# The first chunk's weights and x in two pieces instead of three, x on ScalarE's queue

## What is computed

```python
h = rmsnorm(x, norm1_g)
proj = h @ w_in + b_in                      # 1024 -> 4352 columns
qa, ka, va, qb, kb, vb, ga, gb = split(proj)
oa = neighborhood_attention(qa, ka, va, na_rpb)
ob = sliding_window_gqa(rope(qb), rope(kb), vb, swa_sinks)
merged = sigmoid(ga) * (oa @ w_up_a) + sigmoid(gb) * (ob @ w_up_b)
x = x + merged @ w_out
x = x + moe_clamped_swiglu(rmsnorm(x, norm2_g), ...)   # 32 experts, top 4
return rmsnorm(x, final_g)
```

## Time and profile before

| what | value |
|---|---|
| three timed runs | 1122.39, 1122.46, 1125.32 us |
| median | 1122.46 us |
| the profiled execution's own time | 1121.81 us |
| its span, from the first to the last instruction | 1119.6 us |
| busy in the span | TensorE 1066.8 us (95%), its weight loads 476.0, VectorE 303.2, ScalarE 114.0, GpSimd 43.1 |
| read from HBM | 434.66 MB, 389 GB/s over the span |
| chain that ended last, by engine | TensorE 74%, DMA 17%, SyncE's queue 5% |

### The profile page before, as it was taken

The page is one execution under the profiler, slowest core; times in us unless marked ns, Lnnn a source line. Parts: engine busy times, 40 slices in busy tenths (PEclk is TensorE's granted clock), DMA queues, the critical chain, the costliest instruction groups (busy, mean ns, idle before and its releaser), DMA issues.

```text
span 1119.6 us, 13354 instructions
## 1 busy us (share of the span) xinstructions
PE 1066.8 (95%) x5293; PEld 476.0 (43%) x5293; DVE 303.2 (27%) x656; ACT 114.0 (10%) x243; POOL 43.1 (4%) x44
## 2 busy tenths in 40 slices
PE   8999999999999999999999999999999999999997
PEld 7888888633333333333333333333333333333332
DVE  4356634322222222222222222222121112222213
ACT  1042520200000000000000000000000000000001
POOL 1105500000000000000000000000000000000000
PEclk9999999999999999999999999999999999999999
DMA  9953369599999999999999999999999999999996
GB/s 359 420 209 131 113 241 396 203 384 430 428 428 429 426 429 430 428 426 430 429 428 427 430 429 429 426 430 430 428 427 428 430 428 427 428 430 428 427 425 272
DMA packets 35783, 436.05 MB, mean 389 GB/s; under 512 B 4432, under 2 KB 4944, under 8 KB 6992
## 3 DMA queue, kind: packets, MB, share of 16 engines
q1 hardware_dynamic: 34752, 434.77, 92.8%
q10 hardware_dynamic: 1008, 0.95, 0.3%
HBM read 434.66 MB, written 1.05 MB: 389 GB/s over the span
## 4 chain that ended last, share of the span: by engine, by line
PE 74%; DMA 17%; SPq 5%; DVE 3%; ACT 1%; issue 1%; another core or an unknown queue 0%; POOL 0%; POOLq 0%; DVEq 0%
PE bank L862 29%; DMA ring<-in_w 17%; PE bank L924 16%; PE bank L595 5%; SPq L364 5%; PE bank L836 4%; PE bank L786 4%; PE bank L792 3%; PE bank L696 2%; PE bank L678 2%; PE bank L539 2%; DVE work L1333 2%; PE bank L591 1%; PE bank L764 1%; PE bank L517 1%; PE bank L643 1%
## 5 line engine op out<-in xcount | busy, mean ns | idle before, releaser
L862 PE MATMUL bank<-ring,work 128*64 128x512 f32 x2048 | 450.8, 593 | 18.8 <-DMA ring<-in_w 18.2
L862 PEld LDWEIGHTS bank<-ring,work 128*64 128x64 f32 x2048 | 147.7, 137 | 301.1 <-issue 273.2
L924 PE MATMUL bank<-ring,work 128*64 128x512 f32 x1024 | 234.1, 599 | 18.0 <-DVE work L1333 17.5
L924 PEld LDWEIGHTS bank<-ring,work 128*64 128x64 f32 x1024 | 67.8, 136 | 141.4 <-issue 114.9
L1323 DVE TENSOR_SCALAR work<-bank 128x512 f32<-128x512 f32 x32 | 22.1, 692 | 387.5 <-PE bank L862 387.5
L1505 ACT ACTIVATE work<-work 128x512 f32<-128x512 f32 x32 | 20.1, 630 | 722.4 <-DVE work L1323 722.4
L836 PE MATMUL bank<-work 64*128 64x512 f32 x256 | 63.6, 615 | 0.9 <-DVE work L1303 0.9
L786 PE MATMUL bank<-x2n,work 128*64 128x512 f32 x256 | 61.9, 604 | 0.8 <-DVE work L1238 0.8
L1249 DVE TENSOR_TENSOR work<-bank,vec 128x256 f32<-128x256 f32 x64 | 24.2, 419 | 134.5 <-PE bank L792 134.5
L792 PEld LDWEIGHTS bank<-cst,work 128*128 128x128 f32 x320 | 33.8, 140 | 54.2 <-issue 49.5
L595 PE MATMUL bank<-ring 128*128 128x256 f32 x240 | 54.2, 382 | 0.0
(11 more groups left out here) (194 smaller groups left out, 572.3 us busy)
## 6 DMA issues: line engine op xcount, KB each, us to landing
ring<-in_w SPq DMA_DIRECT2D x184, 2048.0 KB, 40.1
ring<-in_w_in SPq DMA_DIRECT2D x16, 1024.0 KB, 24.0
ring<-in_w SPq DMA_DIRECT2D x15, 1024.0 KB, 13.5
ring<-in_w_out SPq DMA_DIRECT2D x4, 1024.0 KB, 4.8
ring<-in_w_up_a SPq DMA_DIRECT2D x2, 1024.0 KB, 9.4
ring<-in_w_up_b SPq DMA_DIRECT2D x2, 1024.0 KB, 6.1
ring<-in_na_rpb SPq DMA_DIRECT2D x1, 1536.0 KB, 17.9
ring<-in_w SPq DMA_DIRECT2D x2, 512.0 KB, 29.4
```

Of the source, the lines that this page charges most:

```text
L862: last = pe.matmul(bank[CAP * a:CAP * (a + 1), bk, :], kT, pairs[:, pair_of(par, k // 2), at + q * 512:at + (q + 1) * 512], start=False, s ...
L924: last = pe.matmul(bank[CAP * a:CAP * (a + 1), to, :], fT, pairs[:, pair_of(par, c), at + a * 512:at + (a + 1) * 512], start=f == 0, stop= ...
```

## The change

`FIRST` has two slices, row blocks 0 to 3 and 4 to 7, 512 KB of x and 512 KB of weights each. SyncE issues the two pieces of weights only; ScalarE issues the two pieces of x, behind `vec` and ahead of the identity. The semaphores and the waits follow: two pieces for TensorE, VectorE and ScalarE instead of three.

```diff
-        xT_landed = [sem(f"xT_landed{n}") for n in range(3)]
-        first_landed = [sem(f"first_chunk_landed{n}") for n in range(2)]
+        xT_landed = [sem(f"xT_landed{n}") for n in range(2)]
+        first_landed = sem("first_chunk_landed")
...
-        FIRST = [slice(0, 2), slice(2, 4), slice(4, KD)]
+        FIRST = [slice(0, 4), slice(4, KD)]
...
             for n, ks in enumerate(FIRST):
                 cols = slice(ks.start * CW, ks.stop * CW)
-                sp.dma_start(xT[:, ks, :], xT_in[:, ks, :]).then_inc(xT_landed[n], 16)
-                sp.dma_start(ring[:, SLOTS, cols], w_in[0][:, cols]).then_inc(first_landed[n] if n < 2 else landed[SLOTS], 16)
+                sp.dma_start(ring[:, SLOTS, cols], w_in[0][:, cols]).then_inc(landed[SLOTS] if n else first_landed, 16)
...
                 for n, ks in enumerate(FIRST):
-                    pe.wait_ge(first_landed[n] if n < 2 else landed[SLOTS], 16)
+                    pe.wait_ge(landed[SLOTS] if n else first_landed, 16)
...
-                dve.wait_ge(square_done, 3)
+                dve.wait_ge(square_done, 2)
...
             act.dma_start(vec[:], vec_in).then_inc(vec_landed, 16)
+            for n, ks in enumerate(FIRST):
+                act.dma_start(xT[:, ks, :], xT_in[:, ks, :]).then_inc(xT_landed[n], 16)
             act.dma_start(C("ident"), consts[:, CONST["ident"]]).then_inc(ident_landed, 16)
```

## The result

The changed kernel takes 1128.28 us (median of 6 executions, 1127.78 to 1129.03) against 1122.49 us before (6 executions, 1122.39 to 1125.32): a ratio of 1.005, 95% interval 1.004 to 1.006. It is 5.8 us slower, outside the range of the prediction and beyond the 0.3% that I had called the bound of "no change". The profiled execution took 1127.78 us with a span of 1125.6 us, 6.0 us over the span of before.

What follows compares the result with a forecast made beforehand. Bound: the HBM weight stream, whose continuous start hangs on TensorE. The late start's + 1.2 us, other parts nothing, gave 1123.0 by the profiled execution and 1123.7 by the median; forecast 1123.5 us, range 1121.8 to 1125.4.

Steps and rivals of the forecast that it cites:

- The reading of the bound: Whole kernel: a weight stream continuous from 220 us on sets the end, and its start hangs on TensorE.
- the one-for-one reading: TensorE from near 15 us: any shift there arrives at the kernel's end in full.
- Part 2: Start, x on ScalarE's queue behind the gains: x lands at 6.6 us, TensorE starts at 6.95 us, 1.7 us later.
- Both bounds: First x landing: 5.4 us from the identity's 4.2 us, 7.8 us with an even share of 383 GB/s for the rest.
- The rival of the starved queue: First x: ScalarE's queue gets only 90 GB/s, x lands at 10.5 us, TensorE 5.6 us late, 1128 us; chance 0.04.
- Part 3: End of first chunk: the later start costs 0.85 to 1.7 us, depending on when the clock rises; 1.2 us taken.
- Parts 4 and 5: First chunk: second pieces land at 10.2 us without a stall; sum of squares ready at 15.0 us, covered by 2.8 us.
- Part 7: Chunk 1's weights, issued third rather than seventh on SyncE's queue, have the same bytes ahead: cost nothing.
- The last sentence of the rivals: Behind 15 us: later stages stay as they are, since no transfer or instruction there is changed.
- the sum of the bounds: Whole change: + 1.2 us, with bounds of + 0.2 and + 2.9 us.

Runs made afterwards that it cites:

- e8_before_mask_later: GpSimd waits for the scaled hT before its mask additions, against the kernel before: 1122.33 us against 1122.50, ratio 1.000.
- e7_before_warmed: Nine matmuls of ones with unread results on TensorE ahead of the first chunk, against the kernel before: 1121.52 us against 1122.50, ratio 0.9995.

## Why the prediction was wrong, by its own steps

- **The reading of the bound held from 36 us on.** Chunk 1 later by 4.54 us and 1.54 us more behind it are 6.08 us, and the span grew by 6.0. By the prediction's own sign, an end that moves by another amount than the chunk's last matmul, the one-for-one reading from 15 us on was wrong (4.55 against 6.0 us). That TensorE waits for no piece of the first chunk was true of the one execution that had been read. In the profile of `e8_before_mask_later`, whose start is that of the kernel before, the clock rose 3.2 us after the first matmul instead of 5.4, the third weights landed at 11.19 us, and TensorE waited for them (6.0 us in two waits, of which 5.4 are the start).
- **Part 2 failed: its upper bound for the landing of x.** Forecast was x at 6.6 us, bounds 5.4 to 7.8, measured 9.5 us, and the first matmul 4.9 us late instead of 1.7. Both bounds took the identity's 4.2 us as the time after which x's bytes flow. But the identity had ended beside 256 KB of x and 256 KB of weights. In the changed kernel `vec` steps through its 128 packets beside the first weights, 0.5 MB, and x through its own beside the second, 0.5 MB more; so x can't be complete before 1.57 MB have come, not 1.05. In fact more had: 1.66 MB by 7.0 us and 2.23 MB by 8.5 us, when 15 of x's 16 engines had reported, as SyncE's queue began to move 0.34 us sooner and stayed ahead. The last engine adds the rest. The row that says so was there: 86 packets each, 0.18 and 0.66 MB. I had used it for the share of x and not for what stands ahead of x.
- **The rule of the Trainium skill** (page "DMA: Bandwidth & Descriptors", section "Issuing engines are not separate DMA queues") that a second issuer gives no bandwidth agrees with the outcome in its direction, and would have given 6.6 us for x. The same page's section "Queues, rings and completion order", round robin by packet, carries the case: the counts agree with it in all three stretches. The page takes 9 to 17 descriptors for a typical packet. Here the measurement says otherwise: a turn is a single row. An engine has eight rows of the first weights, 0.17 us each (60.7% of 16 engines' 2.2 us over 124 packets), and with all eight in one turn would spend about 1.4 us on them before a row of `vec`. But the weights begin at 1.75 us and `vec` at 2.09 us, and from 2 to 3 us the two move 47 and 33 packets side by side.
- **The rival of the starved queue** had the time, 1128, and x at 10.5 us, with a chance of 0.04 and a mechanism that is not the one found, so its number came true by luck. It took the share of bytes of small packets beside large ones and applied it to x, whose packets are as large as the weights'.
- **Part 3 was nearer its upper end.** The first matmul was 4.90 us late, and of these 4.54 arrived: the slow instructions were 11 instead of 12, since the clock rose 4.7 us after the new start instead of 5.4. In the other executions without the matmuls of ones it rose 3.0 to 5.9 us after the first matmul, and 7 to 14 instructions were slow, so this term alone moves by up to 1.5 us (7 x 0.21) from one execution to another. The prediction calls the step a factor of two in duration and spacing; it is two in the spacing, 0.43 to 0.22 us, and 1.7 in the duration, 634 to 379 ns.
- **Parts 4 and 5 held.** TensorE never waited for the second pieces, and the sum of squares was ready at 14.43 + 3.68 = 18.11 us, 3 us ahead of its use. The second x, though, came at 13.3 us and not at 10.2. **Part 7 held** too: the start of chunk 1 was no wait for its weights.
- **The last sentence of the rivals, that later stages stay as they are, failed.** It put this term at nothing, and it was 1.5 us: a pair of engines that had missed each other by less than 0.1 us. The timeline of before showed GpSimd's additions at 24.22 us and the multiplications' end at 24.19; I had read the multiplications only as a link of TensorE's chain.
- **The range** was too narrow: the sum of the bounds had no term for a later overlap, and the starved queue was left outside it although its condition, a queue loaded beside another, was known to hold.

## What to carry to other kernels

Where a transfer goes to another queue, count the packets ahead of it there, `vec`-like small ones at full count, and price each turn with the bytes that the neighbour queue moves in it. What must land first has to stand first in its queue, and small transfers with one packet per partition belong behind it or beside other small ones. And when one engine's chain is moved by some microseconds, lay it over the other engines' timeline: an overlap that was missed by 0.1 us in one execution is part of the price. A row of a trace is one execution: when the clock rises and when a transfer's last engine reports differ by 1 us and more between two of them.

## What the runs showed of the hardware that I had not expected

- 25 KB in 128 packets took 4.5 us to land as the first of its queue and 7.6 us as the second, beside the second 512 KB of the other queue. From GpSimd's queue they took 6.2 us in 16 packets, the first of which moved 4.5 us after the issue.
- The last of the 16 DMA engines reported up to 1.8 us behind the 15th: 9.54 against 8.49 us for the first x of the changed kernel, 8.90 against 7.14 us for the second weights of `e7_before_warmed`.
- VectorE's multiplications of two SBUF tiles took 1.48 us instead of 0.68 beside GpSimd's additions of two SBUF tiles, and these then started 1.4 us apart instead of 1.0.
- The view of busy time prints a clock of 1.00 also where the trace has no record of it. The first record, at 10.61 us before and at 14.83 us in the changed kernel, marks the step from 634 to 379 ns; nine matmuls of ones ahead of the work moved it to 4.34 us.
